# Two transformer blocks with routed experts on one core: a ring of four buffers for the odd pairs' first pieces

## What is computed

```python
def hier_moe(h, wr_g, br_g, wr_e, br_e, w_gu, w_down):
    p_group = softmax(xf @ wr_g + br_g)                  # 4 groups, top 1
    e_in = logits of the 8 experts of the chosen group   # top 2 of them
    gates = pg * pv / sum(pv)
    return grouped_experts(xf, expert_id, gates, w_gu, w_down)

def expert_block(xb, e):
    a, b = split(xb @ w_gu[e], 2)                        # w_gu[e]: 1024 x 1024
    return (silu(a) * b) @ w_down[e]                     # w_down[e]: 512 x 1024
h = h + hier_moe(rms_norm(h, norm_ffn), ...)
```

## Time and profile before

| | |
|---|---|
| median of 3 runs | 2128.81 us |
| profiled execution | 2130.93 us, its span 2129.1 us |
| busy PE, DVE, ACT, POOL | 94%, 43%, 33%, 4% of the span |
| granted TensorE clock, mean | 0.977 of full speed |
| moved by DMA | 603.71 MB, 284 GB/s over the span |
| layer 0's pairs, first project to last down | 934.83 to 1400.99 us |
| layer 1's pairs | 1652.23 to 2116.97 us |

### The profile page before, as it was taken

One profiled execution on the slowest core, in us unless ns is written; L12 is line 12 of the kernel. 1 busy time (PEld: TensorE's weight loads), 2 busy tenths in 40 slices (PEclk: granted clock), 3 DMA queues, 4 the chain that ended last, 5 costly groups with the idle time before them and its releaser, 6 DMA issues.

```text
span 2129.1 us, 32312 instructions
## 1 busy us (share of the span) xinstructions
PE 1997.3 (94%) x12772; PEld 1449.6 (68%) x12773; DVE 914.6 (43%) x1524; ACT 708.8 (33%) x1109; POOL 80.3 (4%) x119
## 2 busy tenths in 40 slices
PE   7998999999999998889999999999999999999997
PEld 5877899988999897854444444479899444344433
DVE  4876688755653544542222221246555222221212
ACT  3434564254553455521111111144453111111112
POOL 0110211101000200000000000000000000000000
PEclk9999999999999999989999999999998999999999
DMA  9742489802755251479999999935266899999996
GB/s 360 276 145 77 148 300 332 314 30 88 254 189 183 80 172 67 198 317 417 422 422 422 421 422 422 422 123 187 83 214 268 338 422 422 422 422 422 422 422 276
DMA packets 108256, 603.71 MB, mean 284 GB/s; under 512 B 10094, under 2 KB 10548, under 8 KB 59012
## 3 DMA queue, kind: packets, MB, share of 16 engines
q1 hardware_dynamic: 96016, 559.91, 66.5%
q0 software_dynamic: 11872, 42.35, 5.5%
q10 hardware_dynamic: 276, 0.13, 0.0%
HBM read 601.27 MB, written 1.05 MB: 283 GB/s over the span
## 4 chain that ended last, share of the span: by engine, by line
PE 61%; DMA 29%; DVE 4%; ACT 3%; issue 2%; SPq 1%; ACTq 0%; DVEq 0%
DMA expert_w<-in_expert_w_gu 26%; PE bank L1017 11%; PE bank L572 10%; PE bank L574 10%; PE bank L573 10%; PE bank L606 3%; PE bank L1029 3%; PE bank L1002 2%; DMA dense_w<-in_ada_w 1%; PE bank L581 1%; PE bank L583 1%; PE bank L582 1%; PE bank L656 1%; DMA dense_w<-in_w_in 1%; ACT w_high L431 1%
## 5 line engine op out<-in xcount | busy, mean ns | idle before, releaser
L1017 PE MATMUL bank<-expert_w,work 128*64 128x512 f32 (+1 forms) x2240 | 459.8, 599 | 51.6 <-DMA expert_w<-in_expert_w_gu 47.0
L1017 PEld LDWEIGHTS bank<-expert_w,work 128*64 128x64 f32 (+1 forms) x2240 | 153.0, 133 | 352.5 <-issue 352.3
L438 DVE TENSOR_TENSOR w_low<-dense_w,w_high 128x2048 fp32r<-128x2048 f32 x112 | 255.8, 2289 | 216.8 <-ACT w_high L431 216.1
L431 ACT ACTIVATE w_high<-dense_w 128x2048 fp32r<-128x2048 f32 x120 | 228.6, 1910 | 306.0 <-DMA dense_w<-in_mlp_w 186.4
L1029 PE MATMUL bank<-expert_w,work 128*64 128x512 f32 (+1 forms) x1120 | 226.7, 595 | 0.0
L2224 DVE TENSOR_TENSOR work<-work,bank 128x512 f32<-128x512 f32 x32 | 22.0, 687 | 392.2 <-ACT work L1512 392.2
L1029 PEld LDWEIGHTS bank<-expert_w,work 128*64 128x64 f32 (+1 forms) x1120 | 70.0, 132 | 136.4 <-issue 134.3
L1512 ACT ACTIVATE work<-bank 128x512 f32<-128x512 f32 x32 | 19.1, 598 | 429.0 <-PE bank L1017 429.0
L572 PE MATMUL bank<-u_pairs_mlp,w_high 128*128 128x256 f32 x512 | 144.0, 284 | 1.1 <-issue 1.1
L572 PE MATMUL bank<-hidden_pairs,w_high 128*128 128x256 f32 x512 | 144.9, 283 | 0.0
L573 PE MATMUL bank<-hidden_pairs,w_low 128*128 128x256 f32 x512 | 144.9, 283 | 0.0
(11 more groups left out here) (398 smaller groups left out, 3850.2 us busy)
## 6 DMA issues: line engine op xcount, KB each, us to landing
expert_w<-in_expert_w_gu SPq DMA_DIRECT2D x256, 1024.0 KB, 23.0
expert_w<-in_expert_w_down SPq DMA_DIRECT2D x128, 1024.0 KB, 19.2
dense_w<-in_mlp_w SPq DMA_DIRECT2D x64, 1024.0 KB, 5.7
dense_w<-in_ret_w_in SPq DMA_DIRECT2D x24, 1024.0 KB, 5.2
u<-in_ada_w POOLq DMA_DIRECT2D x40, 512.0 KB, 6.7
work<-in_ada_w POOLq DMA_DIRECT2D x40, 512.0 KB, 6.7
dense_w<-in_fox_w_in SPq DMA_DIRECT2D x16, 1024.0 KB, 5.1
dense_w<-in_w_in SPq DMA_DIRECT2D x12, 1024.0 KB, 7.7
```

The lines of the kernel that those rows point to most:

```text
L431: nc.scalar.activation(HIGH_OF[at], dense_w[:, at % RING], ACT.Copy, scale=scale).then_inc(S("w_high_ready"), 1)
L438: ins = nc.vector.tensor_tensor(w_low[:, at % RING], dense_w[:, at % RING], high, ALU.subtract)
L1017: last = mm(free[half][cols, :], rows[:, k, cols], pieces[:, k // 2, a, k % 2, half * 512:(half + 1) * 512], start=k == 0, stop=k == KT - 1)
```

## The change

The first four pieces of every odd pair (groups 0 and 1) go into the four buffers of the dense ring, those of the even pairs stay in `expert_w`. So a pair's groups 0 and 1 can be loaded while the pair before still uses its own. With it:

- SP loads groups 0 and 1 of pair 1 before the loop, and in the round for pair i the groups in the order (i+1, 0), (i+1, 1), (i, 2), (i, 3), (i, 4), (i, 5). Its loop does two pairs per round (7 rounds), and the last groups of pair 15 stand behind it. `ret_in`'s first four pieces are loaded when pair 15 has used the ring's buffers, and `gain_row` likewise.
- Groups 3 and 4 of pair 0 are loaded earlier in layer 0, when two tiles of the attention are done.
- The chosen order of pair 1 is fixed as well (`few[:, 0:2]`), since it is loaded before the swap is known.
- PE runs two nested loops, `Fori(0, 7)` around `Fori(0, 2)`, with one body. In it the first half of project stands twice, once for each buffer, behind a branch on the inner count. Pairs 14 and 15 stand behind the loop, each with its own copy of the body.
- ACT and DVE loop over 15 pairs, and pair 15 stands behind the loop. It makes no gather, no picking matrix and no xg for a pair 16. On PE its order is add_up, turn_hidden, turn_pick, down.

```diff
         def wait_chunk(eng, at):
-            eng.wait_ge(dense_in[at % RING], 16 * (at // RING + 1))
+            eng.wait_ge(dense_in[at % RING], 16 * (at // RING + 1 + (RING_PAIRS if at >= chunk("ret_in", 0, 0) else 0)))
...
             wait_tile(sp, TILES["fox_attn"] + fox_tile(KT - 1, 5))
             for j in range(3):
                 load_experts(0, 0, j)
+            for x in range(2):
+                wait_tile(sp, TILES["fox_attn"] + fox_tile(FOX_HEADS // 2 - 1, x))
+            for j in (3, 4):
+                load_experts(0, 0, j)
             for l in range(DEPTH):
                 wait_tile(sp, TILES["ret_out" if l else "fox_out"] + 7)
-                for j in range(3 if l == 0 else 4, PIECES // 2):
+                for j in range(4 if l else 5, PIECES // 2):
                     load_experts(l, 0, j)
+                for j in range(RING // 2):
+                    load_experts(l, 1, j, 1)
+                sp.wait_ge(S(f"more_known_{l}"), 1)
+                with sp.Fori(0, PAIRS // 2 - 1) as two:
+                    for odd in range(2):
+                        i = 2 * two + 1 + odd
+                        swap = sp.value_load(more_i[0:1, ds(i + 3 * PAIRS, 1)], min_val=0, max_val=1)
+                        swap_next = sp.value_load(more_i[0:1, ds(i + 1 + 3 * PAIRS, 1)], min_val=0, max_val=1)
+                        for j in range(PIECES // 2):
+                            sp.wait_ge(expert_used, PIECES * (PAIRS * l + i - 1) + 2 * j + 2)
+                            if j < RING // 2:
+                                load_experts(l, i + 1, j, odd, swap_next)
+                            else:
+                                load_experts(l, i, j, 0, swap)
...
+                for j in range(RING // 2, PIECES // 2):
+                    sp.wait_ge(expert_used, PIECES * (PAIRS * (l + 1) - 2) + 2 * j + 2)
+                    load_experts(l, PAIRS - 1, j, 0, swap)
+                if l == DEPTH - 1:
+                    sp.wait_ge(expert_used, PIECES * (PAIRS * DEPTH - 1) + 2)
+                    sp.dma_start(gain_row, ...)
                 if l == 0:
                     for j in range(RING):
+                        sp.wait_ge(expert_used, PIECES * (PAIRS - 1) + 2 * (j // 2) + 2)
                         load(chunk("ret_in", 0, j))
-                if l == DEPTH - 1:
-                    sp.dma_start(gain_row, ...)
-                sp.wait_ge(S(f"more_known_{l}"), 1)
-                with sp.Fori(1, PAIRS) as i:
...
+                    if isinstance(odd, int):
+                        for k in range(RING):
+                            row_block(k, odd)
+                    else:
+                        for ring in range(2):
+                            with pe.If(odd == ring):
+                                for k in range(RING):
+                                    row_block(k, ring)
+                    if late is not None:
+                        pe.wait_ge(S("xg_dve"), late)
+                    for k in range(RING, KT):
+                        last = row_block(k, 0)
...
-                with pe.Fori(0, PAIRS) as i:
+                def one_pair(i, two, odd, last=False):
...
+                    if last:
+                        pending(count)
+                        add_up().then_inc(S("added"), 1)
+                        pe.wait_ge(S("hidden_e"), n + 1)
+                        turn_hidden(S("hidden_turned"))
+                        pe.wait_ge(S("pick_w_ready"), n + 1)
+                        turn_pick(pick_w, S("pick_turned"))
+                        pe.wait_ge(S("hidT_ready"), n + 1)
+                    else:
...
+                with pe.Fori(0, PAIRS // 2 - 1) as two:
+                    with pe.Fori(0, 2) as odd:
+                        one_pair(2 * two + odd, two, odd)
+                for odd in range(2):
+                    one_pair(PAIRS - 2 + odd, PAIRS // 2 - 1, odd, last=odd == 1)
```

More of the change, by code:

```diff
@@ L47 @@
 PIECES = KT + 4
+RING_PAIRS = PAIRS // 2
 FURTHER = SEQ // SLOTS - 1
@@ L1007, in experts, with project, row_block @@
                             LARGE: [(slice(UNIT * x, UNIT * (x + 1)), int(x == 3)) for x in range(4)]}
-                def project(rows, loaded, used=None, first=SLOTS, late=None):
-                    for k in range(KT):
-                        if k == KT // 2 and late is not None:
-                            pe.wait_ge(S("xg_dve"), late)
-                        both_in(k, loaded)
+                def project(rows, two, odd, used=None, first=SLOTS, late=None):
+                    def row_block(k, ring):
+                        both_in(k, two, ring if k < RING else odd)
                         for half in range(2):
                             for cols, a in tiles_of[first]:
-                                last = mm(free[half][cols, :], rows[:, k, cols], pieces[:, k // 2, a, k % 2, half * 512:(half + 1) * 512],
+                                last = mm(free[half][cols, :], rows[:, k, cols], piece_of(ring, k // 2, a)[:, k % 2, half * 512:(half + 1) * 512],
                                           start=k == 0, stop=k == KT - 1)
@@ L1020, in project, with down @@
                             last.then_inc(used, 1)
+                        return last
+                    if isinstance(odd, int):
[10 more added lines that the diff above has]
+                        last = row_block(k, 0)
                     return last
-                def down(loaded, used=None, first=SLOTS):
+                def down(two, odd, used=None, first=SLOTS):
                     for f in range(4):
-                        both_in(KT + f, loaded)
+                        both_in(KT + f, two, odd)
                         for half in range(2):
@@ L1102, in experts @@
                                 pe.wait_ge(S(f"more_pick_wT_{l}"), c + 1)
-                                down(loaded).then_inc(S(f"more_down_{l}"), 1)
+                                down(two, odd).then_inc(S(f"more_down_{l}"), 1)
                                 pe.wait_ge(S(f"more_y_act_{l}"), 2 * c + 2)
@@ L1107, in experts @@
                         with pe.If(first_rows == first):
-                            project(xg, loaded, expert_used, first, late=count)
-                    pe.wait_ge(S("pick_ready"), count + 1)
-                    pending(count)
-                    for half in range(2):
-                        gather(half, pick).then_inc(S("gathered"), 1)
-                    pe.wait_ge(S("hidden_e"), n + 1)
-                    turn_hidden(S("hidden_turned"))
-                    pe.wait_ge(S("pick_w_ready"), count)
@@ L1122, in experts @@
                     for first in (SLOTS, LARGE):
                         with pe.If(first_rows == first):
-                            down(loaded, expert_used, first)
+                            down(two, odd, expert_used, first)
+                with pe.Fori(0, PAIRS // 2 - 1) as two:
[3 more added lines that the diff above has]
+                    one_pair(PAIRS - 2 + odd, PAIRS // 2 - 1, odd, last=odd == 1)
@@ L1554, in experts @@
                     take_y(S("y_act"))
+                with act.Fori(0, PAIRS - 1) as i:
+                    one_pair(i)
+                one_pair(PAIRS - 1, last=True)
                 if l == DEPTH - 1:
```

94 lines of the change are left out of this document (57 added, 37 removed).

## The result

The changed kernel takes 2139.84 us, median of 8 runs (2130.25 to 2143.55); the kernel before, timed beside it, 2128.42 us (2124.58 to 2130.39). The ratio is 1.0049, interval 1.0032 to 1.0067: slower by some 10 us, where I forecast no change at 2128.7 us and a range that ended at 2138. The profiled execution took 2138.52 us, span 2136.7, against 2130.93 and 2129.1.

The account below looks back on a forecast made before the run. Each pair was taken to be bound by its piece j=3 landing; gains of 4.5, 5.9 and 2.0 us against code costs of 1.8, 1.8, 2.6, 1.9 and 4.2 summed to -0.1, giving 2128.7 us, range 2113 to 2138.

Parts of the forecast that it names:

- The event that binds a pair: Expert loops: each pair waits for its piece j=3 to land; the new load order gains in pair 15 alone.
- The waits of pair 15: Pair 15's project, both layers: waits for pieces j=2 and j=3 go, -4.5 us.
- project to down: Pair 15, both layers: no gather and adding first cut 6.4 us to 3.4, -5.9 us in all.
- Layer 0's entry: Before layer 0's first pair: data end earlier while the missed code stays, between -4.3 and 0, taken as -2.0 us.
- 88 fetches: PE's code queue q8: about 88 fetches expected as a sign that the prediction is right.
- The loop of eight blocks still fits: Rival on layer 0's loop: eight blocks no longer fit PE's code store, about +120 us, 2250 us; chance 0.11.
- control: Rival: nested loops and ring branches delay first matmuls of some ten pairs, +8 to +12 us, 2139 us; chance 0.07.
- Code stalls hide: Rival: prefetch of PE's code reaches further, only the gains stay, about 2117 us; chance 0.24.
- the code of pairs 14 and 15: Their own code, first run with full queues: +2.6 us in layer 0, +1.9 and +4.2 in layer 1.
- 5.54 us per long skip: PE's branches over a whole unseen code block: each missed jump into a busy queue takes 5.54 us.
- First skip of the large form: First jump over project's large form in each layer: 0 to +1.3 us, booked at +1.8 for both.
- Layer 1's entry: Before layer 1's first pair: jump target now two blocks ahead, 3.4 us with idle queues; 0 to +3.7, taken as +1.8.

Follow-up runs that it names:

- short tail: The changed kernel with the extra rounds and the 96-row forms of project left out of pairs 14 and 15; 2120.64 us, ratio 0.9959.
- the kernel with the lowest ratio: Against the changed kernel: project's forms chosen per half, all 16 pairs in the loop, last gather skipped by a branch; 2117.73 us, ratio 0.9950.
- the second profile: Profile from a repeat of the changed kernel, nothing altered; 2138.39 us, ratio 1.0058.
- artificial stall: The short tail with TensorE made to wait for VectorE's product behind project in pairs 14 and 15; 2134.37 us, ratio 1.0044.
- the peeled pair alone: The kernel before with its last pair taken out of the loop on three engines, without the ring; 2128.76 us, ratio 0.9993.

## Why the prediction was wrong

**Right.** The event that binds a pair is the landing of j=3, and it comes earlier for pair 15 alone: the middle pairs kept their 376 us in layer 0 and 375 in layer 1 (374 after). (My count from 88 to 86 leaves out the two groups that are loaded ahead of the loop; counted with them it stays 88, and the lead is the same.) The waits of pair 15 went, and its project to down is 3.45 us where nothing disturbs it. Together, -10.4 forecast, -11.5 measured in the short tail. Layer 0's entry: -2.0 forecast, -2.3 measured. 88 fetches forecast, 87 counted. The loop of eight blocks still fits (no fetch from 964 to 1340 us), so that rival fell; control was not the cost either, since the same nested loops and ring branches stand in the kernel with the lowest ratio. "Code stalls hide" fell too.

**The step that failed** is the code of pairs 14 and 15, +2.6 in layer 0 and +6.1 in layer 1, 8.7 us in all. Measured against the short tail it is 64.8 - 54.1 = 10.7 and 61.2 - 54.0 = 7.2, 17.9 us (7.7 and 9.4 in the second profile). The term that I put at nothing, without a reason, is the granted clock behind a stall, 9.0 us. The stalls without it come to 17.9 - 9.0 = 8.9 us, near my 8.7, but by luck, since neither their places nor their sizes are mine. Three parts of the step were wrong:

- *The clock.* I priced a stall by its own length. Behind it the granted clock was at half for gather, turns and adding: 2.7 + 0.6 + 1.5 = 4.8 us in layer 0's pair 14, 1.0 in its pair 15, 1.7 + 0.6 + 1.0 = 3.2 in layer 1's pair 14. That is 9.0 us, more than the three gaps themselves (2.50 + 1.78 + 2.78 = 7.1), and enough to turn no change into slower. The profile of before could have warned me. Layer 1's first project takes 16.32 us instead of 13.73, with the clock at 0.50 in its first 4.8 us, and I didn't ask why. And behind layer 0's last down TensorE stood for 2.36 us at 1400.96 us, after a loop at 1.00, and the clock was at 0.80 in the 2 us behind it.
- *The place.* In layer 1 I counted blocks from the header and put full misses at the entries of pairs 14 and 15. One came behind pair 14's project instead, 2.78 us, and pair 15 paid nothing (24.4 us for 24.2 in the short tail); both entries were covered. In layer 0 I had pair 14's place right, but pair 15's stall came behind project and not at the entry. My reading that the next block is always there was wrong too: pair 14's stall in layer 0 is such a block. In layer 1 I also took 2.3 us off for slack; but the slack lies ahead of j=3's landing, and a stall behind it is paid in full.
- *The size.* 5.54 us per long skip became 6.0. In layer 0 I had given 0 to 2.3 us (1.3) to pair 14 and 0 to 1.7 (1.3) to pair 15; the gaps were 2.50 and 1.78.

**First pairs.** "First skip of the large form" +1.8 for both layers: 0.6 + 1.6 = 2.2 in the first profile, but 1.0 + 6.9 = 7.9 in the second, where the clock fell there too. Here code costs even without peeled pairs. **Layer 1's entry:** +1.8 forecast, +0.1 measured; the skip takes 2.66 us, but the gather ahead of it ran at a higher clock (5.82 us for 7.06) and hid the difference. A miss with idle queues takes 2.66 and 2.81 us, where I took 3.4.

With the clock's 9.0 us put in and nothing else changed, my sum of -0.1 gives +9, near the +10 to +11 of the medians; that nearness is partly chance, since the profile that shows the 9.0 us has the change at +5.6. There the code of the last pairs came out 9.2 us above my term and the first pairs 0.4 above, and 3.9 us came out better: the gains by 1.1, layer 0's entry by 0.3, layer 1's by 1.7, the middle pairs by 0.8. Which part of the further 4 to 5 us of the median is which stays open; the second profile (+9.7) puts most of it on layer 1's first pair.

## What to carry to other kernels

A pair taken out of a loop brings its whole code along, what is never run included. The first visit to an unseen block can stop the engine when the data queues are full, after a long jump (1.78 and 2.78 us here) or by running on into it (2.50 us). So keep rare bodies short, or keep the last round in the loop behind a branch. Price a stall of TensorE with what follows it: the gather and adding matmuls here (128 to 512 columns) took up to 1.9 times as long after 2 to 3 us of standing still. And slack only absorbs what comes ahead of the event that binds.

## What the runs showed that I had not expected

- The granted clock behind a stall in a loop that had it at 1.00. Behind each of the six gaps of 2.5 to 2.9 us (changed kernel twice, artificial stall once, pair 14 of both layers) it fell, at the latest some 2 us after the gap's end. Behind shorter gaps it went either way: behind 1.12, 1.81, 2.12 and 2.15 us the gather took 4.99, 6.56, 6.95 and 6.96 us, behind 1.79, 1.81 and 2.41 us (other kernels or executions) 3.76; the adding behind 1.78 us took 2.73, behind 1.72 us 2.15. Even behind 0.71 us (the peeled pair alone, layer 1's first pair) it fell. Down, which follows 10 us later, ran at full clock each time. The runs do not show what decides. The Trainium skill describes matmuls that start at the lower clock again behind waits for DMA in a loop (TensorE: Matmul & The Clock Gate, HAM oscillation — how this bites in real kernels). The trace agrees, and shows it behind a wait for code (0.55) and for VectorE (0.51) too, and behind shorter waits than those of the page's example.
- A jump to unseen code took 2.7 to 2.8 us with idle queues and up to 6.0 with full ones; with the forms of project split, and as many fetches, no stall was left behind project.
- The time to layer 0's first gather varied by 7.5 us (920.4 to 927.9) over kernels whose compute engines run the same code up to there. A change of a few us in one profile has to be read from stages.
